# Holding back the ring's first loads, six products of a zeroed tile, and an output stored in quarters

## The chip, the cores and the metric

The kernel runs on one core of one Trainium2 chip. The metric is the device time of one execution in microseconds; the kernel before takes 2062.8 us, the median of 3 runs (2062.78 to 2063.13).

## The reference

Three blocks follow each other on one activation `x` of 256 tokens and 1024 channels, all in float32:

- block 1: RMS norm, one input projection to 6144 columns (q, k, v, a gate, the recurrence's input and its gate), chunked retention with eight heads, a gated linear recurrence with a causal convolution, and an output projection, then a norm;
- block 2: block attention with relative bias, a convolution, a pooling mixer and a convolved feed-forward part, with layer norms;
- block 3: two layers, each with feed-forward, mixer (an RWKV time mix, then a gMLP), cross attention to a memory and another feed-forward, with a last RMS norm.

For this change two ends matter. The first step of block 1 is

```
xn   = rms_norm(x, norm_in_g)
proj = einsum('btd,de->bte', xn, w_in)
```

and the last of block 3 is `return rms_norm_3(x, final_norm)`, whose 256 x 1024 result is the output.

## The kernel before, in words

**Tiles.** Activations lie with channels on the 128 partitions: `c.h` is 128 x 8 x 256 (8 channel blocks, 256 tokens). All the large weights are cut into *ring units* of 128 x 2048 float32 (1 MB), in the order in which they are used, 282 of them in `stream`. The SBUF tile `c.ring` has 6 slots; unit n goes to slot n % 6. An input projection's unit holds 8 channel blocks of 256 columns and is worked through by `p_unit` (line 252) with 16 products of 128x128 by 128x256. The profile records each float32 product twice, so one unit is 32 records.

**Queues.** SP's queue carries a small piece of the parameters, then the halves of `x` (`x_loaded0`, `x_loaded1`) and the halves of ring unit 0 (`first_half`, `unit_loaded0`) in turn, the rest of the parameters, and units 1 to 5 (lines 2772 to 2780). Behind them a loop refills slot after slot, each time waiting for `unit_done` (line 2785), and at the end SP stores `c.h` as the output in two halves (line 2789), each when half of the final norm's four vector instructions are done. ScalarE's queue loads the norm's constants first (`common_loaded`, line 2794), and, behind the squares of `x`, the other constants, the gate weights and the decay table (lines 2800 to 2802). GpSimd's queue loads two small tables (lines 2823, 2824).

**The order of the head.** DVE writes three constants (`c.eps`, line 999) and zeroes the head of a padded tile (line 1000, semaphore `b1_pad`, for which ScalarE's first activation waits too). When a half of `x` is there, DVE multiplies it by the norm's gain (`gain_blocks`, line 425) and ScalarE squares it (line 350). PE waits for `common_loaded`, and `norm_units` then runs `first_unit` (line 271): the products of unit 0 on the gained but not yet normalised `x`, channel block by channel block, each when its block is there; the second half of unit 0 is waited for at block 4. Then `rms_tensor` sums the squares (line 393, semaphore `sq_added` from DVE's line 418), and `p_unit` works through unit 1, also on the gained `x`. While it runs, ScalarE and DVE make the reciprocal root and the normalised `xn`; units 2 and 3 read `xn`. The results of units 0 and 1 are rescaled by DVE (line 458), which waits for the parameters first (`par_loaded`).

**PE's order** is written out by hand in `b1_tensor`, `b2_tensor` and `b3_tensor`. `c.hid`, a 128 x 2 x 512 tile, is first used in block 1 some units later, and PSUM bank 7 (`c.ps[:, 7, :]`) first by the recurrence's gates.

**The tail.** `b3_vector` multiplies by the last reciprocal root in four instructions of two channel blocks each (line 2751), each incrementing `xn_ready`; SP's two stores wait for the second and the fourth.

Of the kernel before, what the change touches and what calls it, by code (L numbers as in the profile page):

```python
# [20 lines left out]
P = 128  # L21
T = 256
# [213 lines left out]
def p_unit(c, pe, n, q, x, j=None, token_major=False, between=None):  # L236


    c.wait_loaded(pe, n, j)
    if q >= BANKS:  # L240
        c.wait_read(pe, q - BANKS, j)
    w = c.ring[:, n % UNITS, :].rearrange("p (k n) -> p k n", k=KB)
    out = c.bank(q).rearrange("p (m t) -> p m t", m=2)
    for m in range(2):
        if m and between:
            between()
        for k in range(KB):
            if token_major:
                mm = c.nc.tensor.matmul(out[:, m, :], x[:, k, m * P:m * P + P], w[:, k, :],  # L249
                                        start=k == 0, stop=k == KB - 1)  # L250
            else:
                mm = c.nc.tensor.matmul(out[:, m, :], w[:, k, m * P:m * P + P], x[:, k, :],  # L252
                                        start=k == 0, stop=k == KB - 1)
    mm.then_inc(c.S[f"unit_done{n % UNITS}"], 1)
# [37 lines left out]
def norm_units(c, pe, name, k):  # L292


    n0, q0 = PLAN[name]
    first_unit(c, pe, n0, q0, c.xg, c.S["xg_ready"], 8 * GAINED.index(k))
    rms_tensor(c, pe, NK[k])
    p_unit(c, pe, n0 + 1, q0 + 1, c.xg)
    pe.wait_ge(c.S["xn_ready"], 8 * NK[k] + 8)
# [500 lines left out]
NK = {name: i for i, name in enumerate(NORMS)}  # L800
# [92 lines left out]

def b1_tensor(c, pe):
    S, nc, W = c.S, c.nc, c.work
    pe.wait_ge(S["common_loaded"], 16)
    norm_units(c, pe, "b1_xlru", "b1_in")
    for u in range(2, 4):
        n0, q0 = PLAN["b1_xlru"]
        p_unit(c, pe, n0 + u, q0 + u, c.xn)  # L900
    n0, q0 = PLAN["b1_q"]
    pe.wait_ge(S["con_loaded"], 16)
    pe.wait_ge(S["relb_loaded"], 32)
    nc.tensor.matmul(c.ps[0:8, 5, 0:384], c.relb[0:32, :], c.c("bucket_hot")[0:32, :], start=True, stop=True)\
        .then_inc(S["b2_bias_mm"], 1)

    def lru_gates(n):
        if n == 0:
            pe.wait_ge(S["decay_loaded"], 32)
        pe.wait_ge(S["b1_conv"], n + 1)  # L910
        if n >= 2:
            pe.wait_ge(S["b1_gate_i"], n - 1)
        for g in range(2):
            mm = nc.tensor.matmul(c.ps[:, 6 + n % 2, g * T:g * T + T], c.gates[:, g, n, :], W[5][:, n, :],
                                  start=True, stop=True)
        mm.then_inc(S["b1_gate_mm"], 1)

    for u in range(8):
        p_unit(c, pe, n0 + u, q0 + u, c.xn)
        if u >= 5:  # L920
            lru_gates(u - 5)
    n0, q1 = PLAN["b1_v"]
    for u in range(4):
        p_unit(c, pe, n0 + u, q1 + u, c.xn, token_major=True)
        lru_gates(u + 3)
    lru_gates(7)
    ng, qg = PLAN["b1_gret"]
    v = W[2][:, :, :].rearrange("p a b -> p (a b)").rearrange("p (m n) -> p m n", m=2)
    prob = c.hid[:, :, :].rearrange("p a b -> p (a b)").rearrange("p (a b) -> p a b", a=2)
    pe.wait_ge(S["b1_rotated"], 8)  # L930
    pe.wait_ge(S["b2_bias_read"], 1)

    def scores(p):
        if p > 0:
            pe.wait_ge(S["b1_prob"], 2 * p)
        for e in range(2):
            hd = 2 * p + e
            nc.tensor.matmul(c.ps[:, 4 + e, 0:T], W[1][:, hd, 0:P], W[0][:, hd, :], start=True, stop=True)
            nc.tensor.matmul(c.ps[:, 4 + e, T:T + P], W[1][:, hd, P:T], W[0][:, hd, P:T],
                             start=True, stop=True).then_inc(S["b1_scores"], 1)  # L940

    def outputs(p):
        if p == 0:
            pe.wait_ge(S["b1_gate_i"], 8)
            c.wait_read(pe, q1 + 3)
            c.wait_read(pe, q1 + 2)
        else:
            pe.wait_ge(S["b1_o_read"], p)
        for e in range(2):
            hd = 2 * p + e  # L950
            pe.wait_ge(S["b1_prob"], hd + 1)
            nc.tensor.matmul(c.ps[:, 6, e * T:e * T + T], v[:, 0, hd * P:hd * P + P],
                             prob[:, e, 0:T], start=True, stop=False, skip_group_check=True)
            mm = nc.tensor.matmul(c.ps[:, 6, e * T + P:e * T + T], v[:, 1, hd * P:hd * P + P],
                                  prob[:, e, T:T + P], start=False, stop=True, skip_group_check=True)
        mm.then_inc(S["b1_o"], 1)

    def means(p):
        pe.wait_ge(S["b1_o_read"], p + 1)
        if p > 0:  # L960
            pe.wait_ge(S["b1_var_read"], p)
        nc.tensor.matmul(c.ps[:, 7, :], c.c("mean_p"), c.t1[:, 0, :], start=True, stop=True)\
            .then_inc(S["b1_mean"], 1)

    def variances(p):
        pe.wait_ge(S["b1_cen_sq"], p + 1)
        nc.tensor.matmul(c.ps[:, 7, :], c.c("mean_p"), c.t1[:, 1, :], start=True, stop=True)\
            .then_inc(S["b1_var"], 1)

    def gate_unit(u, between=None):  # L970
        p_unit(c, pe, ng + u, qg + u, c.xn, between=between)

    scores(0)
    gate_unit(0)
    gate_unit(1)
    outputs(0)
    for p in range(1, 4):
        scores(p)
        means(p - 1)
        gate_unit(2 * p)  # L980
        variances(p - 1)
        if p < 3:
            gate_unit(2 * p + 1)
        outputs(p)
    gate_unit(7, lambda: means(3))
    variances(3)
    n0, _ = PLAN["b1_out"]
    for u in range(8):
        pe.wait_ge(S["b1_y"] if u < 4 else S["b1_y_lru"], u % 4 + 1)
        src = W[0] if u < 4 else W[7]  # L990
        d_unit(c, pe, n0 + u, lambda k: src[:, 2 * (u % 4) + k, :], u == 0, u == 7,
               before_fourth=(lambda: pe.wait_ge(S["b1_var_read"], 4)) if u == 0 else None)


def b1_vector(c, dve, ch):
    S, nc, W = c.S, c.nc, c.work
    v = nc.vector
    for i, e in enumerate((EPS, 1e-5, 64e-5)):
        ch.step(v.memset(c.eps[:, i:i + 1], e))
    v.memset(c.pad[:, :, 0:4], 0.0).then_inc(S["b1_pad"], 1)  # L1000
    dve.wait_ge(S["b1_pad"], 1)
    for b in range(4):
# [89 lines left out]
    _, qg = PLAN["b1_gret"]  # L1092
# [1669 lines left out]
def build(nc, x, params, consts, late_consts, stream, decay, gates, rel_bias, w_pool, bias_rows, mem, lora1,  # L2762
          lora_wa, lora_g, spatial, spatial_b, out):
    with ExitStack() as ctx:
        c = Ctx(nc, ctx, None)
        S = c.S
# [3 lines left out]
        @block.sync  # L2770
        def _(sp):
            sp.dma_start(c.par[:, 0:8], params[:, 0:8]).then_inc(S["x_loaded0"], 16)
            for i in range(2):
                sp.dma_start(c.h[:, 4 * i:4 * i + 4, :], x[:, 4 * i:4 * i + 4, :]).then_inc(S[f"x_loaded{i}"], 16)
                sp.dma_start(c.ring[:, 0, 1024 * i:1024 * i + 1024], stream[0, :, 1024 * i:1024 * i + 1024])\
                    .then_inc(S["unit_loaded0" if i else "first_half"], 16)
            sp.dma_start(c.par[:, 8:N_PARAMS], params[:, 8:N_PARAMS]).then_inc(S["par_loaded"], 16)

            for s in range(1, UNITS):
                sp.dma_start(c.ring[:, s, :], stream[s]).then_inc(S[f"unit_loaded{s}"], 16)  # L2780
            with sp.Fori(1, N_UNITS // UNITS) as r:
                for s in range(UNITS):
                    unit = sp.snap(r * UNITS + s)
                    sp.wait_ge(S[f"unit_done{s}"], r)
                    sp.dma_start(c.ring[:, s, :], stream[bass.ds(unit, 1)].rearrange("a p n -> (a p) n"))\
                        .then_inc(S[f"unit_loaded{s}"], 16)
            for i in range(2):
                sp.wait_ge(S["xn_ready"], 8 * NK["final"] + 2 * i + 2)
                sp.dma_start(out[:, 4 * i:4 * i + 4, :], c.h[:, 4 * i:4 * i + 4, :]).then_inc(S["out_stored"], 16)
            sp.wait_ge(S["out_stored"], 32)  # L2790

        @block.scalar
        def _(act):
# [14 lines left out]
        @block.tensor  # L2808
        def _(pe):
            b1_tensor(c, pe)  # L2810
            b2_tensor(c, pe)
            b3_tensor(c, pe)

        @block.vector
        def _(dve):
            ch = Chain(dve, S["vector_step"])
            b1_vector(c, dve, ch)
            b2_vector(c, dve, ch)
            b3_vector(c, dve, ch)
# [140 lines left out]
```

## Time and profile before

| | |
|---|---|
| median of 3 runs | 2062.8 us |
| profiled execution | 2062.13 us, its span 2060.3 us |
| mean granted clock of TensorE in it | 0.997 |
| PE (matmul) busy | 2019.7 us, 98% |
| DVE busy | 1126.8 us, 55% |
| GpSimd busy | 1014.8 us, 49% |
| DMA, mean over the span | 149 GB/s, 307.65 MB |
| ring units | 275 issues of 1024 KB in the profile, median 4.8 us from issue to landing |

Times in the profile count from the start of the span. PE is the TensorE matmul row, PEld its weight loads, which overlap it. A busy PE is not PE at its peak, since matmuls are pipelined and their ends are modelled. The granted clock is given as a share of 2.4 GHz.

### The profile page before, as it was taken

How to read it: one execution, taken by the hardware profiler on the slowest of the kernel's cores; microseconds unless marked ns; L12 is line 12 of the kernel's file. 1: busy time of each engine (PE TensorE's matmuls, PEld its weight loads, DVE VectorE, ACT ScalarE, POOL GpSimd, SP SyncE). 2: the span in 40 equal slices, each digit the busy share in tenths (PEclk: the TensorE clock that was granted, in tenths of full speed). 3: DMA queues.
4: the chain of work that ended last, by engine and by line, in shares of the span. 5: the costliest groups of instructions: out<-in, count | busy, mean ns of one | idle time of the engine just before them, and what ended most of it. 6: DMA issues, size and time to landing. Idle time of an engine off the chain costs nothing.

```text
span 2060.3 us, 39608 instructions
## 1 busy us (share of the span) xinstructions
PE 2019.7 (98%) x17062; PEld 1899.6 (92%) x17062; DVE 1126.8 (55%) x1958; ACT 375.0 (18%) x777; POOL 1014.8 (49%) x775
## 2 busy tenths in 40 slices
PE   8999999999999999999889999999999999999998
PEld 7888887899998999978788999999999999989998
DVE  3635134456515675336757577726773455576752
ACT  1343012133201000023421210001000231120000
POOL 0000000258753888400001568885888677547884
PEclk9999999999999999999999999999999999999999
DMA  8634443344443444523002244444444544434441
GB/s 330 170 127 153 143 164 115 134 166 172 164 166 127 175 167 164 190 102 120 26 5 102 103 164 164 169 175 155 175 167 164 205 161 148 151 115 164 167 175 68
DMA packets 43879, 307.65 MB, mean 149 GB/s; under 512 B 5288, under 2 KB 5544, under 8 KB 7744
## 3 DMA queue, kind: packets, MB, share of 16 engines
q1 hardware_dynamic: 40752, 291.78, 39.4%
q0 software_dynamic: 2096, 7.31, 1.4%
q10 hardware_dynamic: 864, 6.10, 0.7%
q8 instruction: 134, 2.20, 0.4%
q14 instruction: 33, 0.27, 0.1%
HBM read 302.54 MB, written 2.62 MB: 148 GB/s over the span
## 4 chain that ended last, share of the span: by engine, by line
PE 91%; DVE 7%; issue 1%; ACT 1%; DMA 0%; DVEq 0%; SPq 0%
PE ps L584 56%; PE ps L252 15%; PE ps L311 5%; PE ps L249 3%; PE ps L271 1%; PE ps L286 1%; DVE sb_work L425 1%; PE ps L1676 1%; DVE sb_xn L2539 1%; DVE sb_work L418 1%; PE ps L1652 1%; PE ps L393 0%; DVE sb_h L785 0%; PE ps L2268 0%; PE ps L2121 0%
## 5 line engine op out<-in xcount | busy, mean ns | idle before, releaser
L584 PE MATMUL ps<-sb_work,sb_ring 128*128 128x128 f32 x3968 | 475.9, 275 | 1.7 <-ACT sb_work L1724 1.4
L584 PEld LDWEIGHTS ps<-sb_work,sb_ring 128*128 128x128 f32 x3968 | 459.1, 192 | 2.6 <-ACT sb_work L1724 2.2
L555 POOL TENSOR_TENSOR sb_table<-sb_ring 128x512 f32<-128x512 f32 x126 | 161.4, 1281 | 372.0 <-PE ps L584 190.0
L584 PE MATMUL ps<-sb_work,sb_table 128*128 128x128 f32 x2256 | 285.4, 275 | 0.0
L584 PEld LDWEIGHTS ps<-sb_work,sb_table 128*128 128x128 f32 x2256 | 268.4, 192 | 0.0
L558 POOL TENSOR_TENSOR sb_ring<-sb_ring 128x512 f32<-128x512 f32 x189 | 260.4, 1378 | 0.0
L557 POOL TENSOR_TENSOR sb_table<-sb_table,sb_ring 128x512 f32<-128x512 f32 x126 | 176.1, 1398 | 9.9
L584 PE MATMUL ps<-sb_xn,sb_ring 128*128 128x128 f32 x1440 | 175.5, 275 | 0.0
L584 PEld LDWEIGHTS ps<-sb_xn,sb_ring 128*128 128x128 f32 x1440 | 168.6, 192 | 0.4
L560 POOL TENSOR_TENSOR sb_table<-sb_ring,sb_table 128x512 f32<-128x512 f32 x126 | 168.4, 1337 | 0.0
L252 PE MATMUL ps<-sb_work,sb_ring 128*128 128x256 f32 x736 | 162.8, 380 | 0.0
L555 POOL TENSOR_TENSOR sb_pad<-sb_ring 128x512 f32<-128x512 f32 x63 | 80.6, 1279 | 162.3 <-PE ps L584 114.8
L252 PEld LDWEIGHTS ps<-sb_work,sb_ring 128*128 128x128 f32 x736 | 139.4, 190 | 20.5 <-issue 1.7
L584 PE MATMUL ps<-sb_work,sb_pad 128*128 128x128 f32 x1144 | 144.3, 275 | 0.0
L584 PEld LDWEIGHTS ps<-sb_work,sb_pad 128*128 128x128 f32 x1144 | 135.9, 192 | 0.0
L252 PE MATMUL ps<-sb_xn,sb_ring 128*128 128x256 f32 x576 | 126.4, 379 | 0.0
L252 PEld LDWEIGHTS ps<-sb_xn,sb_ring 128*128 128x128 f32 x576 | 109.2, 190 | 17.9 <-issue 3.5
L701 DVE TENSOR_TENSOR sb_t<-ps,sb_std 128x256 f32<-128x256 f32 x73 | 30.5, 417 | 147.6 <-ACT sb_std L655 147.6
L311 PE MATMUL ps<-sb_work,sb_ring 128*128 128x256 f32 x480 | 104.3, 379 | 0.8 <-DVE sb_work L2691 0.8
L311 PEld LDWEIGHTS ps<-sb_work,sb_ring 128*128 128x128 f32 x480 | 91.0, 190 | 14.1 <-DVE sb_work L2691 1.2
L655 ACT ACTIVATE sb_std<-ps 128x128 f32<-128x128 f32 x75 | 20.7, 276 | 415.2 <-PE ps L584 415.2
L557 POOL TENSOR_TENSOR sb_pad<-sb_pad,sb_ring 128x512 f32<-128x512 f32 x63 | 87.1, 1382 | 4.9
(442 smaller groups left out, 2911.9 us busy)
## 6 DMA issues: line engine op xcount, KB each, us to landing
sb_ring<-stream SPq DMA_DIRECT2D x275, 1024.0 KB, 4.8
sb_table<-decay ACTq DMA_DIRECT2D x1, 1536.0 KB, 20.9
bias_rows<-sb_relg POOLq DMA_DIRECT2D x1, 1536.0 KB, 34.7
sb_con<-consts ACTq DMA_DIRECT2D x1, 1216.0 KB, 10.2
sb_table<-lora POOLq DMA_DIRECT2D x1, 1152.0 KB, 6.0
sb_h<-x SPq DMA_DIRECT2D x2, 512.0 KB, 6.3
sb_ring<-stream SPq DMA_DIRECT2D x2, 512.0 KB, 7.9
sb_work<-gates ACTq DMA_DIRECT2D x1, 1024.0 KB, 14.8
```

The lines of the kernel that those rows point to most:

```text
L249: mm = c.nc.tensor.matmul(out[:, m, :], x[:, k, m * P:m * P + P], w[:, k, :], start=k == 0, stop=k == KB - 1)
L252: mm = c.nc.tensor.matmul(out[:, m, :], w[:, k, m * P:m * P + P], x[:, k, :], start=k == 0, stop=k == KB - 1)
L271: mm = c.nc.tensor.matmul(c.bank(q)[:, m * T:m * T + T], w[:, k, m * P:m * P + P], x[:, k, :], start=k == 0 and m == 0, stop=k == KB - 1, ...
L286: mm = c.nc.tensor.matmul(c.bank(q + u)[:, m * T:m * T + T], w[:, k, m * P:m * P + P], x[:, k, :], start=k == 0 and m == 0, stop=k == KB - ...
L311: mm = c.nc.tensor.matmul(c.ps[:, 4 + m // 2, (m % 2) * T:(m % 2) * T + T], w[:, k, m * P:m * P + P], x2(k), start=first and k == 0 and m ...
L555: v.tensor_tensor(s[:, 0], a[1][0], a[1][1], ALU.add).then_inc(S["fw_ready"], 1)
L557: v.tensor_tensor(s[:, 1], s[:, 0], a[0][0], ALU.subtract).then_inc(S["fw_ready"], 1)
L558: v.tensor_tensor(a[1][0], a[0][0], a[1][0], ALU.subtract).then_inc(S["fw_ready"], 1)
L560: v.tensor_tensor(s[:, 2], a[0][1], s[:, 1], ALU.subtract).then_inc(S["fw_ready"], 1)
L584: ins = mm(fast_bank(c, g, b)[:, i * P:i * P + P], *(sides[::-1] if token_major else sides), start=first and i == 0 and j == 0, stop=last ...
L655: c.nc.scalar.activation(first_product(c, g), fast_bank(c, g, 0)[:, 0:P], ACT.Copy).then_inc(c.S["fast_p1"], 1)
L701: ch.step(v.tensor_tensor(out.rearrange("p (a t) -> p a t", a=4)[:, 0:4:3, :], two[:, P:3 * P].rearrange("p (a t) -> p a t", a=2), p1, ALU ...
```

## The change

PE starts with six products of a tile of zeros into PSUM bank 7, ahead of its wait for the norm's constants; DVE zeroes 384 columns of `c.hid` for them. SP waits for the whole of unit 0 before it asks for the rest of the parameters and for units 1 to 5. The output goes out in four stores of two channel blocks in place of two stores of four.

```
 def b1_tensor(c, pe):
     S, nc, W = c.S, c.nc, c.work
+    pe.wait_ge(S["b1_pad"], 1)
+    for _ in range(6):
+        nc.tensor.matmul(c.ps[:, 7, 0:T], c.hid[:, 0, 0:P], c.hid[:, 0, P:P + T], start=True, stop=True)
     pe.wait_ge(S["common_loaded"], 16)
...
     for i, e in enumerate((EPS, 1e-5, 64e-5)):
         ch.step(v.memset(c.eps[:, i:i + 1], e))
+    ch.step(v.memset(c.hid[:, 0, 0:384], 0.0))
     v.memset(c.pad[:, :, 0:4], 0.0).then_inc(S["b1_pad"], 1)
...
+            sp.wait_ge(S["unit_loaded0"], 16)
             sp.dma_start(c.par[:, 8:N_PARAMS], params[:, 8:N_PARAMS]).then_inc(S["par_loaded"], 16)
...
-            for i in range(2):
-                sp.wait_ge(S["xn_ready"], 8 * NK["final"] + 2 * i + 2)
-                sp.dma_start(out[:, 4 * i:4 * i + 4, :], c.h[:, 4 * i:4 * i + 4, :]).then_inc(S["out_stored"], 16)
-            sp.wait_ge(S["out_stored"], 32)
+            for i in range(4):
+                sp.wait_ge(S["xn_ready"], 8 * NK["final"] + i + 1)
+                sp.dma_start(out[:, 2 * i:2 * i + 2, :], c.h[:, 2 * i:2 * i + 2, :]).then_inc(S["out_stored"], 16)
+            sp.wait_ge(S["out_stored"], 64)
```

## Rows read from the trace of the kernel before

**Rows 1.** The page, busy time by engine and the chain that ended last by engine

```profile
PE 2019.7 (98%) x17062; PEld 1899.6 (92%) x17062; DVE 1126.8 (55%) x1958; ACT 375.0 (18%) x777; POOL 1014.8 (49%) x775
...
PE 91%; DVE 7%; issue 1%; ACT 1%; DMA 0%; DVEq 0%; SPq 0%
```

**Rows 2.** The chain of waits, first 60 us: start us, us, what

```profile
1.68 6.82 DMA sb_ring<-stream
...
8.59 8.86 PE ps L271 x32
17.45 0.86 PE ps L393 x4
```

**Rows 3.** The timeline: start us, us, engine, line, what [idle before]

```profile
8.59 8.86 PE L271 MATMUL ps<-sb_work,sb_ring 128*128 128x256 f32 x32 [8.59 <-DMA sb_ring<-stream]
...
18.15 7.07 PE L252 MATMUL ps<-sb_work,sb_ring 128*128 128x256 f32 x32
```

**Rows 4.** PE by stretch: us, PE busy (records), granted clock, DMA share, GB/s

```profile
8.59:12.03 3.44, 3.44 (x8) 1.00 1.04 428
12.03:15.47 3.44, 3.44 (x17) 1.00 1.03 436
```

**Rows 5.** Timeline's issues, and DMA issues one at a time: KB, us to landing

```profile
2.62 0.49 SPq L2775 DMA_DIRECT2D sb_ring<-stream  x1
...
sb_ring<-stream SPq DMA_DIRECT2D x1, 512.0 KB, 9.1
...
3.86 0.69 SPq L2780 DMA_DIRECT2D sb_ring<-stream  x1
...
sb_ring<-stream SPq DMA_DIRECT2D x1, 1024.0 KB, 11.3
...
4.59 0.82 SPq L2780 DMA_DIRECT2D sb_ring<-stream  x1
...
sb_ring<-stream SPq DMA_DIRECT2D x1, 1024.0 KB, 16.0
...
5.45 0.49 SPq L2780 DMA_DIRECT2D sb_ring<-stream  x1
...
sb_ring<-stream SPq DMA_DIRECT2D x1, 1024.0 KB, 20.2
...
10.43 0.34 ACTq L2800 DMA_DIRECT2D sb_con<-consts  x1
...
sb_par<-params SPq DMA_DIRECT2D x1, 4.0 KB, 2.1
...
sb_table<-decay ACTq DMA_DIRECT2D x1, 1536.0 KB, 20.9
```

**Rows 6.** The timeline of DVE in the head

```profile
1.20 0.09 DVE L1000 MEMSET sb_pad<- 128x32 f32 x1
...
5.58 1.14 DVE L425 TENSOR_SCALAR sb_work<-sb_h,sb_par 128x256 f32<-128x256 f32 x4 [4.30 <-DMA sb_h<-x]
...
10.42 1.14 DVE L425 TENSOR_SCALAR sb_work<-sb_h,sb_par 128x256 f32<-128x256 f32 x4 [3.70 <-DMA sb_h<-x]
```

**Rows 7.** All engines by stretch, PE, PEld, DVE, ACT, POOL, then as rows 4

```profile
2.00:9.00 7.00, 0.41 (x1) 0.44 (x2) 1.14 (x4) 1.83 (x4) 0.51 (x1) 1.00 0.96 300
9.00:14.00 5.00, 5.00 (x17) 4.10 (x17) 3.12 (x7) 1.15 (x2) 0.00 (x0) 1.00 1.03 430
```

**Rows 8.** The timeline and the DMA issues of the tail

```profile
2054.70 2.48 DVE L2751 TENSOR_TENSOR sb_h<-sb_work,ps 128x512 f32<-128x512 f32 x4 [1.31 <-PE ps L385]
2056.02 1.54 SPq L2789 DMA_DIRECT2D out<-sb_h  x2
...
out<-sb_h SPq DMA_DIRECT2D x2, 512.0 KB, 2.7
```

**Rows 9.** A stretch by engine as in rows 7, and PE's waits

```profile
865.40:872.20 6.80, 4.85 (x13) 3.87 (x14) 5.07 (x13) 0.04 (x1) 0.78 (x2) 0.50 0.94 349
...
PE ps L329 <- DVE sb_work L2691: 1.7, 1, 1.7
```

## The prediction

> **What bounds the kernel now.** I read the page first. PE is busy for 98% of the span and holds 91% of the chain that ended last; DVE has 7% and DMA rounds to 0% [rows 1]. So almost nothing of the 2060.3 us is open to this change: it touches the head, before PE is running without a break, and the tail, after PE has finished. A microsecond is worth a microsecond there, because the chain runs over PE from the head to the end.
>
> The chain of the first 60 us comes next [rows 2]. The chain waits 6.82 us for the first half of ring unit 0, which is asked for at 1.68 and lands at 8.5; PE then works through unit 0 (8.59 to 17.45), four products for the norm (to 18.3) and ring unit 1. No later DMA appears: each other load is in time today. Every microsecond by which *unit 1's products* start earlier than 18.15 [rows 3] is gained, and nothing else in the head counts.
>
> Unit 0 is slow for its work: 32 records take 8.86 us where the same 32 of unit 1 take 7.07 [rows 3]. Two equal windows show why: 8 records in the first 3.44 us and 17 in the next [rows 4]. The granted clock reads 1.00 in both, but 0.43 us a record against 0.2 is the engine at the lower of its two levels (1.2 and 2.4 GHz) for its first 3.4 us after the idle start.
>
> The issues show how the loads queue [rows 5]. SP asks for x half, ring half, x half, ring half; DVE's first passes show x's halves landed by 5.5 and 10.4 [rows 6]; unit 0's halves are there at 8.5 and at 2.62 + 9.1 = 11.7. Unit 1 lands at 3.86 + 11.3 = 15.2. Units 2 and 3 land at 20.6 and 25.7, 5.1 to 5.4 us apart, because ScalarE's queue feeds 3776 KB of constants, gates and decay (asked for from 10.43 on; the decay, asked for last and within a microsecond of the first, takes 20.9 us to land, near 32) to the same DMA engines. The 16 engines are full from 2 us on, but move only 300 GB/s until 9 us and 430 after it [rows 7].
>
> At the tail DVE writes the result in four instructions, 2.48 us from 2054.70 on; SP stores halves at 2056.02 and about 2057.2, and each takes 2.7 us to land [rows 8], so the second lands near 2059.9 and the span ends 0.4 us later.
>
> **Part 1, the zeroed tile and six products.** The memset of 128x384 stands ahead of b1_pad. The nearest rows are 85 ns for 128x32 and 0.29 us for each of four DVE passes over 128x256 [rows 6], so 0.1 to 0.5 us. DVE and ACT wait for x until 5.5, which hides it; uncovered it would cost those 0.1 to 0.5. The six products are 12 records and start near 1.8. At 0.43 us each they end at 7.0; if the clock rises after 8 of them, 8 x 0.43 + 4 x 0.22 = 4.3 us, at 6.1. I take 6.5. Unit 0 then runs with its clock up: 7.07 in place of 8.86, 1.8 us less. Nothing before executes products of zeros, so the bounds of this term are 0 and 1.8.
>
> The Trainium skill ("TensorE: Matmul & The Clock Gate", the section on the HAM clock gate) says that the gate follows how busy the array has been, and that unthrottling needs activity alone; by that, zeros count and the term is 1.8. No run here shows it. The sum below is the same by either reading.
>
> **Part 2, SP waits for unit 0 before it asks for the rest.** Queued behind the wait on SP are the 244 KB of parameters, ring units 1 to 5, and the refill loop. Two effects, of opposite sign.
>
> (a) What it may hasten: the four needed loads. Let S be the start of unit 0's products, L the landing of its second half (now 8.59 and 11.7). Lower bound: a 512 KB transfer with nothing else in flight takes 2.7 us [rows 8], so x's first half lands at 3.9 and the next three 1.2 us apart (512 KB at 430 GB/s) at 5.1, 6.3, 7.5. Upper bound: nothing is hastened, L = 11.7. In between: x, unit 0, the common constants and w_pool are 2.36 MB, and at the rates seen they have all been moved by 9.6 us (7 us at 300 GB/s are 2.10 MB to 9.0, then 430 GB/s); so the last landing at 11.7 has later loads' packets ahead of it on some engines. I take L = 10.2, between 9.9 and 11.7 and towards the first, and S = 7.5 (the products of zeros end before it).
>
> (b) What it costs: unit 1 is asked for after L in place of 3.86. SP wakes, issues the parameters (0.5 us; its other issues take 0.49 to 0.82), then unit 1; from issue to first byte is about 1 us (a 4 KB load takes 2.1 us to landing [rows 5]). Unit 1's own 1024 KB take 2.4 us alone (430 GB/s) and 5.1 to 5.4 beside ScalarE's queue. That queue is there: its loads start with x's second half, about 1.3 us ahead of L, and are over 20 us from done. Sum: L + 0.1 + 0.5 + 1.1 + 5.3 + 0.2 = L + 7.2, with bounds L + 4.3 (not shared) and L + 7.6. With L = 10.2: 17.4, bounds 14.5 and 17.8.
>
> PE needs unit 1 at S + 7.07 + 0.86 = S + 7.9 less the overlap of the pipelined records, 7.76 = 15.3. So **the ring takes the place of the clock as what ends last**: PE stands for about 2.1 us before unit 1, and the term of part 1 vanishes inside this wait (with no clock gain PE would be ready at 17.1, still before 17.4). Unit 1 starts at 17.4 in place of 18.15: **-0.75 us**. At the bounds of L it is 7.5 + 7.2 = 14.7 (-3.5) and 18.9 (+0.75); break-even is L = 10.95.
>
> Behind unit 1: unit 2 lands 5.4 later, 22.8, needed at 17.4 + 6.9 = 24.3; unit 3 at 28.2 against 31.2; then the constants' queue is empty. The refill loop starts when SP has issued unit 5, at about L + 4, and unit 0 is free only near 14.4. The parameters (needed by DVE at 23.4) land near 12.5; con, gates and decay are asked for no later than now. No second stall: unit 2 would have to land over 1.5 us later than this before it cost anything.
>
> **Part 3, output in quarters.** Now the second half is asked for after DVE's last instruction (near 2057.2) and takes 2.7 us. In quarters the last one is asked for at the same instant, but has 256 KB in place of 512: at 430 GB/s 0.6 us less, provided the earlier quarters are through. They are: DVE's steps are 0.62 apart (four in 2.48) and a quarter takes 0.62. Four issues of 0.35 us fit between DVE's steps. Bounds: 0 (if pieces of 2 KB per partition move at half the rate; 0.6 us each becomes 1.2 and they queue) and -0.7. I take **-0.6**.
>
> **Sum.** Against the profiled execution (2062.1 us: span 2060.3 and 1.8 around it) -0.75 - 0.6 = -1.35 gives 2060.8. The median of the runs shown is 2062.8, 0.7 above the profiled one, so the median forecast is **2061.4 us**. Own range 2060.0 to 2062.6, L from 8.8 to 10.9 and the store's bounds. A measurement of this kernel tells 0.2% (4.1 us) from no change; this isn't that.
>
> **Rivals.**
> *Nothing hastened* (L stays 11.7): for it, the DMA engines are full from 2 us [rows 6], and one queue serves its loads in the order asked (unit 1, 2, 3 land in that order [rows 5]), so later ones should not stand in front. Unit 1 at 18.9: +0.75 - 0.6 = +0.15, 2062.9. Against it, the sum of bytes above. The Trainium skill ("DMA: Bandwidth & Descriptors", the section on queues, rings and completion order) says that on each of the 16 engines descriptors are consumed in ring order; by that, holding later loads back frees nothing on an engine that has not reached them, which is this rival. The trace's one order of landings agrees; it does not show the engines one by one.
> *Unit 1 in time*: if it doesn't share with ScalarE's queue it lands at L + 4.3 = 14.5, PE never stands, and the whole gain shows: unit 1 at 15.3, -2.85 - 0.6 = -3.45, 2059.3; with S at 6.5 it is ready at 14.3 and starts at 14.5, 2058.5. Against it, the 5.1 to 5.4 us spacing of units 2 and 3.
> *Slower: the clock falls in the new wait.* The granted clock was 0.50 from 865.4 to 872.2 [rows 9], in a stretch of PE waits between a norm's products, so it does come down in mid-kernel. If PE stands before unit 1 for 2 us or more and the clock falls, unit 1's products repeat unit 0's slow start, +1.8. With L = 11.7: +0.75 + 1.8 - 0.6 = +1.95, 2064.8. It decides if a wait of that length is enough. No row settles that: behind the head the longest single wait of PE is 1.7 us [rows 9], and the clock reads 0.50 in one stretch before the tail.
> *The products do nothing for the clock*: no separate time, as worked out, except that it then can't fall either: 2061.4.
>
> **Chances.** Forecast 0.46 (with the last rival inside it), nothing hastened 0.22, unit 1 in time 0.14, clock falls 0.13, anything else (the lower-clock stretch at 865 moving with the new timing, up to 2 us either way) 0.05. Range 2058.7 to 2064.3: it reaches into both outer cases. Faster by over 0.2% needs under 2058.7: half of the in-time case, 0.08. Slower by over 0.2% needs over 2066.9: 0.04. Within: 0.88.
>
> **What would show it.** Right: unit 0's 32 records in about 7 us; a PE wait of 1 to 3 us for a ring DMA ahead of the first L252 products, which start between 16.5 and 18.2; units 1 and 2 landing over 5 us apart; four stores, the last landing about 2.1 us after its issue. Wrong: no wait for the ring there (the in-time rival), or L252's first records at 0.4 us (the clock rival), or a landing of unit 0 unmoved from 11.7. A median outside 2060.0 to 2062.6 with all these signs present would mean that the stream behind unit 3 is not simply shifted.

## The result, and the profile after

The changed kernel takes 2072.95 us (median of 5 runs, 2070.77 to 2073.31) against 2062.8 before (5 runs, 2061.3 to 2069.4): slower, at a ratio of 1.0040 with a 95% interval of 1.0029 to 1.0051. Of the 2062.8 us that is 10 us, small but clear of the noise. Its profiled execution is the fastest of the five, 2070.8 us with a span of 2069.0, 8.7 above before's 2060.3. The forecast was 2061.4.

The chain of waits of the changed kernel, first 80 us (start us, us, what), has two loads in it where before had one [rows 2]:

```profile
2.63 9.47 DMA sb_ring<-stream
12.10 0.02 issue
12.12 0.33 SPq L2782
12.45 0.04 issue
12.49 13.35 DMA sb_ring<-stream
25.84 0.04 issue
25.88 22.36 PE ps L252 x96
```

Unit 0's second half lands at 12.10, not hastened (11.7 before [rows 5]). SP then asks for the parameters and, at 12.49, for unit 1, which takes **13.35 us** to land. PE's timeline puts unit 1's products at 25.88, where they stood at 18.15 [rows 3]:

```profile
1.87 4.29 PE L898 MATMUL ps<-sb_hid 128*128 128x256 f32 x12 [1.87 <-DVE sb_pad L1004]
...
9.65 9.81 PE L271 MATMUL ps<-sb_work,sb_ring 128*128 128x256 f32 x32 [3.49 <-DMA sb_ring<-stream]
...
25.88 8.55 PE L252 MATMUL ps<-sb_work,sb_ring 128*128 128x256 f32 x32 [5.55 <-DMA sb_ring<-stream]
```

PE is idle 3.49 us ahead of unit 0 and 5.55 ahead of unit 1. Behind each gap the unit's 32 records run slow: 9.81 and 8.55 us. The stretches (us, PE busy and records, PEld, DVE, ACT, POOL, granted clock, DMA share, GB/s) show the clock that goes with it:

```profile
6.20:9.60 3.40, 0.00 (x0) 0.00 (x0) 0.47 (x2) 0.40 (x1) 0.00 (x0) 0.80 0.87 300
9.65:13.06 3.41, 3.41 (x8) 2.78 (x9) 2.08 (x6) 1.16 (x2) 0.00 (x0) 0.50 0.42 98
...
20.30:25.80 5.50, 0.03 (x1) 0.00 (x0) 4.83 (x10) 0.48 (x1) 0.00 (x0) 0.95 1.01 427
25.88:29.30 3.42, 3.42 (x9) 2.79 (x10) 0.22 (x1) 0.00 (x0) 0.00 (x0) 0.59 1.00 422
29.30:32.70 3.40, 3.40 (x17) 3.01 (x16) 0.00 (x0) 0.00 (x0) 0.00 (x0) 1.00 1.02 424
```

The products of zeros had raised the clock (12 records in 4.29 us); it fell during PE's idle stretch to 9.6, was at 0.50 when unit 0 began, and fell again in the wait ahead of unit 1. Two more stretches show the DMA engines far from full around SP's wait, busy for 0.37 and 0.76 of their time, where before had 0.96 up to 9 us and 1.03 behind it [rows 7]:

```profile
10.00:12.00 2.00, 2.00 (x6) 1.55 (x6) 1.13 (x5) 1.13 (x2) 0.00 (x0) 0.50 0.37 72
12.00:14.00 2.00, 2.00 (x6) 1.60 (x5) 1.79 (x4) 0.02 (x1) 0.00 (x0) 0.50 0.76 268
```

The single DMA issues (KB, us to landing; the issue times are in the lines between) tell what stood beside unit 1:

```profile
10.88 0.33 ACTq L2805 DMA_DIRECT2D sb_con<-consts  x1
...
sb_con<-consts ACTq DMA_DIRECT2D x1, 1216.0 KB, 5.7
...
sb_table<-decay ACTq DMA_DIRECT2D x1, 1536.0 KB, 14.3
...
12.12 0.33 SPq L2782 DMA_DIRECT2D sb_par<-params  x1
...
sb_par<-params SPq DMA_DIRECT2D x1, 244.0 KB, 8.4
...
12.49 0.59 SPq L2785 DMA_DIRECT2D sb_ring<-stream  x1
...
sb_ring<-stream SPq DMA_DIRECT2D x1, 1024.0 KB, 13.3
```

The 244 KB of parameters take 8.4 us and land at 20.5; unit 1, behind them in SP's queue, lands at 25.84, and the decay table near 26. So all of the 3776 KB of ScalarE's queue moved ahead of unit 1 or beside it.

The DMA packets tell how (queue q1 is SP's, q10 ScalarE's; packets, MB, share of the 16 engines' time), in three stretches, from 12.15 to 15.6, from 16 to 18 and from 20 to 24 us:

```profile
q10 hardware_dynamic: 122, 1.12, 80.6%
...
q10 hardware_dynamic: 90, 0.70, 83.2%
q1 hardware_dynamic: 76, 0.15, 19.0%
...
q10 hardware_dynamic: 85, 0.98, 57.6%
q1 hardware_dynamic: 89, 0.72, 42.7%
```

In the first stretch nothing of SP's queue moves, though the parameters were asked for at 12.12: their first packet starts at 15.62, when the 128 packets of ScalarE's constants are all but through (the last starts at 15.81). Then the two queues go nearly packet for packet, whatever a packet holds: one of 1952 bytes for the parameters against one of 8192 for the gates in the second stretch, 8192 for unit 1 against 12288 for the decay table in the third. Parameters and unit 1 have 128 packets each; unit 1's first starts at 18.69.

At the tail, the last quarter takes as long as the last half did [rows 8]:

```profile
2063.30 2.48 DVE L2755 TENSOR_TENSOR sb_h<-sb_work,ps 128x512 f32<-128x512 f32 x4 [0.84 <-PE ps L385]
...
2065.81 0.33 SPq L2794 DMA_DIRECT2D out<-sb_h  x1
out<-sb_h SPq DMA_DIRECT2D x1, 256.0 KB, 2.8
```

**The account of the 8.7 us.** Unit 1's products start 7.73 later and take 1.48 longer (8.55 against 7.07): +9.2 when units 2 and 3 begin (34.27 against 25.06). The long run of 1736 records of L584 starts at 431.98 against 422.78, +9.2 still, and DVE's instructions, matched one by one with before's, are 9.1 later from 1100 us on, so the middle of the kernel in the main just shifts. At 2063.30 DVE's output starts 8.6 later than 2054.70; the half microsecond between is the last norm, behind whose products DVE idles 0.84 us in place of 1.31 [rows 8]; four of them took 0.75 us in place of 1.22, as the clock fell only behind them, at 2063.0. From there to the end it is 5.7 us against 5.6.

### The profile page after: what moved, and what is told of

Its sections match the earlier page's. It is cut to its first block, busy times and chain, and to the rows that moved or that the text cites. A ratio compares the mean times of both kernels' runs of the same rounds, so it can differ in the third digit from the quotient of the medians.

```text
span 2069.0 us, 39635 instructions
## 1 busy us (share of the span) xinstructions
PE 2026.8 (98%) x17074; PEld 1904.3 (92%) x17074; DVE 1126.9 (54%) x1959; ACT 375.4 (18%) x777; POOL 1015.7 (49%) x775
## 4 chain that ended last, share of the span: by engine, by line
PE 90%; DVE 6%; issue 1%; DMA 1%; ACT 1%; SPq 0%; DVEq 0%
PE ps L584 56%; PE ps L252 15%; PE ps L311 5%; PE ps L249 3%; DMA sb_ring<-stream 1%; PE ps L271 1%; PE ps L286 1%; DVE sb_work L425 1%; PE ps L1680 1%; DVE sb_xn L2543 1%; DVE sb_work L418 1%; PE ps L1656 1%; PE ps L393 0%; DVE sb_h L785 0%; PE ps L2272 0%
## 5 line engine op out<-in xcount | busy, mean ns | idle before, releaser
L584 PE MATMUL ps<-sb_work,sb_ring 128*128 128x128 f32 x3968 | 475.9, 275 | 1.7 <-ACT sb_work L1728 1.4
L584 PEld LDWEIGHTS ps<-sb_work,sb_ring 128*128 128x128 f32 x3968 | 459.1, 192 | 2.6 <-ACT sb_work L1728 2.2
L584 PE MATMUL ps<-sb_work,sb_table 128*128 128x128 f32 x2256 | 285.4, 275 | 0.0
L584 PEld LDWEIGHTS ps<-sb_work,sb_table 128*128 128x128 f32 x2256 | 268.4, 192 | 0.0
L584 PE MATMUL ps<-sb_xn,sb_ring 128*128 128x128 f32 x1440 | 175.5, 275 | 0.0
L584 PEld LDWEIGHTS ps<-sb_xn,sb_ring 128*128 128x128 f32 x1440 | 168.6, 192 | 0.4
L584 PE MATMUL ps<-sb_work,sb_pad 128*128 128x128 f32 x1144 | 144.2, 275 | 0.0
L584 PEld LDWEIGHTS ps<-sb_work,sb_pad 128*128 128x128 f32 x1144 | 135.9, 192 | 0.0
```

The source lines that it names most:

```text
L584: ins = mm(fast_bank(c, g, b)[:, i * P:i * P + P], *(sides[::-1] if token_major else sides), start=first and i == 0 and j == 0, stop=last ...
```

## The experiments

Two theories stood against each other: SP's wait makes unit 1 late; or the products of zeros do the harm. The first four kernels ran on one chip, where before had a median of 2064.7 us over 21 runs; the next four on another (2063.3, 35 runs), the last three on a third (2062.9, 27 runs). Every ratio is against before on its own chip, with the 95% interval.

**The wait alone.**

```
 (kernel before)
+            sp.wait_ge(S["unit_loaded0"], 16)
             sp.dma_start(c.par[:, 8:N_PARAMS], ...)
```

> The kernel before plus SP's wait for unit 0 alone. Theory 1 (the wait makes unit 1 late): unit 1 lands at 25 to 26 us, PE stands 6 to 8 us ahead of its products, the clock falls in that wait, and the time is 8 to 10 us above before (2071 to 2073). Theory 2 (the products of zeros do the harm, by holding up the loads of unit 0 or by letting the clock fall before it): at most 2 us above before.

2075.6 us (2075.3 to 2082.0), ratio 1.0058 (1.0045 to 1.0072). From PE's timeline, in a trace of the slowest of the five executions:

```profile
9.45 9.85 PE L271 MATMUL ps<-sb_work,sb_ring 128*128 128x256 f32 x32 [9.45 <-DMA sb_ring<-stream]
...
26.12 10.07 PE L252 MATMUL ps<-sb_work,sb_ring 128*128 128x256 f32 x32 [5.95 <-DMA sb_ring<-stream]
```

Unit 1 starts at 26.1, PE stands 5.95 us, and its products take 10.07 us. The wait alone does the whole harm; theory 2 falls. The time is 2.6 us over my span of 2071 to 2073, of which before's time on this chip explains 1.9; against that before it is 10.9 us slower, a little more than the 8 to 10 expected. In the trace units 2 and 3 begin 11.0 us late (36.02), which fits the median; the rest of that execution's 20 us was lost far behind the head, most of it between 1050 and 1080 us of before's time, and says nothing of the wait.

**The change without the wait.**

```
 (changed kernel)
-            sp.wait_ge(S["unit_loaded0"], 16)
```

> The changed kernel without SP's wait. Theory 1: unit 1 is in time again and at most the clock's gain of unit 0 (0 to 1.8 us) shows: 2061 to 2063. Theory 2: most of the loss stays, over 2067.

2062.8 us (2060.3 to 2067.8), ratio 0.9995 (0.9985 to 1.0005). All of the loss is gone, as theory 1 has it. PE's timeline and its stretches (columns as above):

```profile
1.87 5.40 PE L898 MATMUL ps<-sb_hid 128*128 128x256 f32 x12 [1.87 <-DVE sb_pad L1004]
7.11 7.23 PE L271 MATMUL ps<-sb_work,sb_ring 128*128 128x256 f32 x32
...
15.03 7.07 PE L252 MATMUL ps<-sb_work,sb_ring 128*128 128x256 f32 x32
...
7.11:10.55 3.44, 3.44 (x17) 2.85 (x16) 1.27 (x5) 1.15 (x2) 0.00 (x0) 1.00 1.03 385
```

Here the first half of unit 0 was there before the products of zeros had ended, and unit 0 ran at the upper level from its first record (17 in 3.44 us, against 8 [rows 4]). Products of zeros count for the clock. PE's work on unit 1 starts 3.1 us earlier than before, yet the span is 2061.0, 0.7 longer. The five longest pieces of the chain show where it went; this is the kernel without the wait

```profile
663.85 193.87 PE ps L584 x1736
1205.41 193.86 PE ps L584 x1736
```

and this the kernel before:

```profile
667.11 193.87 PE ps L584 x1736
1205.61 193.87 PE ps L584 x1736
```

3.3 us ahead at 664, 0.2 ahead at 1205. Between them lies the stretch in which the granted clock dips [rows 9]. From 858 to 886 it reads 0.82 in the kernel without the wait

```profile
858.00:886.00 28.00, 25.61 (x116) 22.35 (x116) 23.68 (x61) 2.09 (x4) 2.51 (x4) 0.82 0.45 164
```

and 0.88 in the kernel before:

```profile
858.00:886.00 28.00, 25.24 (x136) 22.43 (x135) 21.48 (x55) 2.36 (x5) 2.50 (x4) 0.88 0.42 146
```

But the longer dip took little. DVE's instructions, matched one by one in the two traces, are 3.3 us ahead up to 855 us of before's time, 2.8 ahead behind the dip, 2.0 ahead at 1050 and 0.2 at 1080. Most went between 1050 and 1080, in the RWKV time mix's many small products, where the clock reads 1.00 in both. PE stops there for spells in which the profile shows nothing that it waits for ("issue"), 4.2 us in all from 1045 to 1081 against 2.8 before; why is not shown, and no experiment was made on it. The last norm took another 0.8 us. There the granted clock fell at 2051.6, so that eight products of the norm took 1.87 us in place of 1.05; before, it fell only at 2053.2, behind them.

**The parameters ahead of the wait.**

```
 (changed kernel)
-            sp.wait_ge(S["unit_loaded0"], 16)
             sp.dma_start(c.par[:, 8:N_PARAMS], ...)
+            sp.wait_ge(S["unit_loaded0"], 16)
```

> The changed kernel with the parameters asked for ahead of SP's wait, so that only ring units 1 to 5 wait. Theory 1a (the parameters' 128 small pieces alternate one by one with the large pieces of ScalarE's queue, which held unit 1 back by 3 to 5 us): unit 1 lands at about 21 to 22.5 us and the time falls by 3 to 5 us against the changed kernel, to 2067 to 2070. Theory 1b (unit 1 is late because the bytes of ScalarE's queue stand ahead of it, whatever SP asks for first): under 1 us better than the changed kernel.

2070.8 us (2069.4 to 2071.9), ratio 1.0034 (1.0021 to 1.0048). The chain:

```profile
11.92 10.16 DMA sb_ring<-stream
22.09 0.04 issue
22.13 24.03 PE ps L252 x96
```

Unit 1 lands at 22.1, 10.2 us behind unit 0 in place of 13.7. Theory 1a holds for the landing: 3.5 us of it was the parameters, a quarter of a unit's bytes in as many packets as a whole one. The rest stays: unit 1, now first behind the wait, is asked for at 11.92, and its first packet starts at 15.62, again when ScalarE's constants are all but through. The time missed what was expected, 3 to 5 us less and 2067 to 2070: by the medians it fell by 2.1 us against the changed kernel, which was measured beside another before (2062.8). Unit 1's products, 10.22 us long here, took 1.7 back, so units 2 and 3 begin at 32.19 against 34.27, and by 1100 us only 0.3 of these 2.1 is left.

**The output in quarters alone.**

```
 (kernel before)
-            for i in range(2):      # two stores of four channel blocks
+            for i in range(4):      # four stores of two channel blocks
```

> The kernel before with the output stored in quarters alone. By the trace of the changed kernel, the last landing comes 5.28 us after DVE's first output instruction, 5.25 before: no difference, within 0.3 us of before. By the prediction's term: 0.6 us faster.

2064.5 us (2062.8 to 2069.3), ratio 1.0003 (0.9994 to 1.0012). No gain; the interval leaves room for 1.2 us, so it is the trace that says the term is zero. The output has landed 5.22 us behind the start of DVE's first output instruction, 5.23 in before; in the changed kernel it is 5.3 (2.51 + 2.8).

**ScalarE's three loads behind unit 1.**

```
 (changed kernel, the wait kept)
+            act.wait_ge(S["unit_loaded1"], 16)
             act.dma_start(c.con[:, N_COMMON:...], ...)      # then gates and decay
```

> The changed kernel with ScalarE's three large loads asked for only when ring unit 1 has landed. If unit 1 is late by sharing the DMA engines with ScalarE's queue, it lands about 4.5 to 5 us after unit 0 (near 17 us), PE hardly stands ahead of it, and the time is 2062 to 2065. If it is late by SP's wait itself (issue and first byte), it lands after 20 us and the time stays over 2067.

2061.1 us (2059.5 to 2064.7), ratio 0.9987 (0.9977 to 0.9996). The chain:

```profile
2.62 8.41 DMA sb_ring<-stream
...
11.41 4.99 DMA sb_ring<-stream
16.40 0.04 issue
16.45 20.99 PE ps L252 x96
```

Unit 1 lands 4.99 us after its issue and 5.4 after unit 0, and PE waits 0.51 us for it. With SP's wait in place, taking ScalarE's queue out of the way removes the whole loss of 10 us, and the time is a little below the 2062 to 2065 expected. So what made the wait dear was ScalarE's queue, ahead of unit 1 and beside it.

**Twelve products of zeros; GpSimd's loads held back; both.**

```
 (kernel before, with the memset)
+    for _ in range(12):      # in place of none
...
 (kernel before)
+            pool.wait_ge(S["unit_loaded0"], 16)
             pool.dma_start(c.relb[0:32, :], rel_bias)      # then w_pool
```

> The kernel before with twelve products of zeros ahead of unit 0, no wait on SP, output in halves. In the changed kernel six products ended at 6.2 us, the granted clock fell at 8.2 and unit 0 started at the lower level. Twelve reach to about 8.7 us, where unit 0 starts. Theory (the gap is what lost the clock): unit 0's 32 records take 7.0 to 7.2 us in place of 8.86, 1.5 to 1.9 us faster than before. Rival (the engine is at the lower level for its first products on real data in any case): 0 to 0.3 us slower than before.

> The kernel before with GpSimd's two small loads asked for only after unit 0 has landed. In both traces the first half of unit 0 is on 15 of its 16 engines 1.7 to 2.5 us before the last. If GpSimd's loads hold that one back, unit 0's first half lands by 7.2 us and its second by 10.5, and the time falls by 1.2 to 1.6 us. If not, both landings stay within 0.5 us of 8.5 and 11.7 and so does the time.

> Both of the two before together. If both are right the gains add but for the products of zeros, which end at 8.7 us and then set the start of unit 0: 1.6 to 2 us faster than before. If only the products are right, as they are alone.

Twelve products: 2062.6 us (2060.0 to 2063.2), 0.9992 (0.9983 to 1.0002); unit 0 took 7.07 us in its trace, as the theory has it, and starts at 8.85. GpSimd's loads held back: 2063.3 (2059.9 to 2064.9), 0.9996 (0.9987 to 1.0006). Both: 2062.8 (2060.7 to 2066.7), 1.0000 (0.9989 to 1.0011). None of the three shows the gain that was expected of it; the intervals leave room for all three gains, so they are not excluded either. In the two traces with GpSimd's loads held back unit 0's first half landed at 6.9 and 7.1 and its second at 10.5 and 10.4, as expected if these loads are in the way; of the eleven traces without, ten have it between 7.8 and 9.6 and one, the changed kernel without the wait, at 6.9. That speaks for GpSimd's loads as a cause but doesn't show it, since the landing can be as early with them.

**Is holding back ScalarE's loads good by itself?** With the wait gone from the changed kernel (first), the same without the hold (second), and the hold alone on the kernel before (third).

> The changed kernel without SP's wait, and with ScalarE's three large loads asked for only when ring unit 1 has landed. In both kernels without SP's wait so far unit 1 landed in time, so holding ScalarE's loads should change PE's start on unit 1 by nothing: within 1 us of the next kernel. If holding them back is good by itself (the rival to 'it only repairs what SP's wait broke'), it is 1 to 2 us faster than the next kernel.

> The changed kernel without SP's wait once more, on the chip of its neighbours. Theory: 0 to 2 us faster than before, as unit 0 starts warmer, with the rest given back where the granted clock dips later.

> The kernel before with ScalarE's three large loads asked for only when ring unit 1 has landed, and nothing else. Theory (in the kernel before unit 1 is not what ends last): within 0.5 us of before. Rival: 1 to 2 us faster.

2061.6 us (2059.0 to 2063.8), 0.9995 (0.9986 to 1.0004); 2060.05 (2058.9 to 2061.8), 0.9988 (0.9979 to 0.9997); 2062.6 (2059.6 to 2064.0), 0.9998 (0.9989 to 1.0007). The hold gains nothing by itself; it only repairs what SP's wait broke. The first is even 1.5 us slower than the second, where at most 1 was expected; 0.8 of it stands in the traces already at unit 0, whose first half landed that much later, and the rest is open. The changed kernel without the wait is the fastest here, 2.8 us under before's median on this chip, more than the 0 to 2 expected, but its first series gave 0.9995: by the two together it is between equal and 0.1% faster, and it beats the changed kernel by some 10 us.

## Why the prediction was wrong

**What held.** The head sets unit 1's start, PE carries nearly every microsecond of it to the end in the changed kernel, and the ring's load takes the place of the clock as what ends last. For the profiled execution the sum gave 2060.8 us and 2070.8 was measured. Of these 10 us, 6.5 are one term, unit 1's landing behind L; 1.9 are L itself (12.1 for 10.2), 1.5 the clock ahead of unit 1 and 0.6 the quarters, less 0.5 in the last norm.

**The term that failed** is "L + 0.1 + 0.5 + 1.1 + 5.3 + 0.2 = L + 7.2". This is the step that turned a forecast gain into a loss: what SP's loads cost once they are asked for behind ScalarE's. Measured: L + 13.7, which is 3.5 us to the first packet of SP's queue, 3.1 more to the first of unit 1, and 7.1 from there to its landing. The sum had 1.7, nothing and 5.5.
- About 1.1 us to the first byte is the price with nothing else asked for: with ScalarE's loads held back the parameters' first packet started 1.0 us after their issue. Here ScalarE's constants, asked for at 10.88, were ahead, and SP's queue moved nothing for 3.5 us; with the parameters asked for first, unit 1 had to wait 3.7 us for its own first packet.
- The parameters were given their issue time and no share of the engines. I counted their bytes and put their landing near 12.5; it was 20.5. Their 128 packets went nearly packet for packet with 8192-byte ones of ScalarE's queue, which is the alternation of theory 1a. They took 8.4 us beside that queue and 2.6 without it.
- The 5.3 us for unit 1 beside ScalarE's queue was read off units 2 and 3 [rows 5], behind a queue that was already moving. From its first packet unit 1 took 7.1 us here and 6.5 with the parameters asked for first.
- With ScalarE's queue out of the way all of it together is L + 5.4, so that queue cost 8.4 us.

**L was not hastened.** I took 10.2, by a sum of bytes. With SP's wait, unit 0's second half landed at 12.1, 12.2, 11.9 and 11.0; without it at 10.4 to 11.8 in nine traces, before's 11.7 among them. So the rival "nothing hastened" was right about L (the full engines that it cites as rows 6 stand in rows 7), though not about the time, 2062.9, since it shared the failed term. The Trainium skill ("DMA: Bandwidth & Descriptors", the section on queues, rings and completion order) has it that an engine takes its descriptors in ring order; these landings agree with what the prediction made of that.

**The clock rival came true, twice.** It was priced at 1.8 us and given 0.13. The clock fell in the wait ahead of unit 1: its products took 1.48 us more in the changed kernel, and about 3.0 more in two other traces (10.07 us with the wait alone, 10.22 with the parameters first). It also fell between the products of zeros and unit 0, which I had not considered: PE was idle for 3.49 us there, unit 0 took 9.81 us against 8.86, and the products bought nothing. My forecast took S = 7.5, and so saw only a gap of 1 us; gaps of 1.0 to 1.5 us did no harm in three traces (unit 0 in 7.14 to 7.15 us).

**The products** ended at 6.16, the lower of my two ends, and count for the clock, as the Trainium skill's page "TensorE: Matmul & The Clock Gate" (the HAM clock gate) led me to expect; unit 0 in 7.23 and 7.07 us bears it out. The 1.8 us of this term were right for unit 0 where no long gap follows.

**The quarters** were given 0.6 us and gave none: the last one's bytes are fewer, but from issue to landing it takes 2.8 us against 2.7. Three quarters in front of it and pieces of half the size stand where the sum had one half; which of the two it is, no run tells apart.

**The range** left out the upper end because L + 7.6 was taken for a bound. A queue with 3776 KB in it was named in the same paragraph; all of it ahead of unit 1, at 430 GB/s, is 9.0 us. With 2.4 for unit 1 and the 1.9 of the other terms that is L + 13.3, an estimate from the rows of before that comes near what was measured.

## What to carry to other kernels

A wait in front of a load is priced by all that other queues can put ahead of it in the meantime, not by its own bytes; a first upper estimate is everything already asked for, its own queue included. Small transfers beside a queue of large ones were priced here by their number of packets more than by their bytes; it helped to ask for them before the wait. Products that only keep the clock up can serve only if they reach the first real one: six of them followed by 3.5 us of idling gained nothing, and with a gap of at most 1.5 us they took 1.6 to 1.8 us off unit 0. Whether that reaches the end of the kernel is another matter: the whole kernel's gain was between nothing and 0.1%.

## What the runs showed of the hardware that was not expected

- A load asked for 1.2 us behind another queue's 1216 KB moved no packet for 3.5 us, until those were all but through. After that the two queues went nearly packet for packet. So 244 KB in 128 rows of 1952 bytes took 8.4 us to land beside a queue of large packets, and 2.6 us in the kernel in which that queue was held back; the unit behind it took 5.0:

```profile
sb_par<-params SPq DMA_DIRECT2D x1, 244.0 KB, 2.6
...
sb_ring<-stream SPq DMA_DIRECT2D x1, 1024.0 KB, 5.0
```

- A gain at the head did not reach the end whole: 3.3 us ahead at 664 became 0.2 at 1205, most of it lost between 1050 and 1080 with the clock at 1.00. The same code, run again on another chip, ended 2.8 us ahead of before in the medians.
